# A causal decoder layer in float32: later gate/up tiles in pairs, two of eight k pairs by seven block products

## The chip, the cores and the metric

One core of a Trainium2 chip runs the whole program once. The metric is the device time of an execution in microseconds. Three timed runs of the kernel before gave 953.26, 953.99 and 954.17 us; their median is 953.99 us. The profile is of a further execution.

## The reference

One layer is computed for 256 tokens of width 2048, in float32: a sparse attention mixer, then a gated feed-forward part, each followed by a layer norm over a weighted residual (alpha = 2^0.25). The change concerns the feed-forward part:

```
x <- LN(alpha*x + mixer(x))
x <- LN(alpha*x + (silu(x @ w_gate) * (x @ w_up)) @ w_down)
x: 256 x 2048, w_gate, w_up: 2048 x 5632, w_down: 5632 x 2048
```

## The kernel before, in words

**Split products.** TensorE multiplies numbers of the reduced type fp32r. To keep float32 precision each operand is a high part (rounded to fp32r) plus a low part (the rest), and a product is three matmuls: high by high, high by weight low, low by weight high (`product`, L1324; L1327 is the matmul). The activations are split once and lie in `act_t` (index 0 high, 1 low). The weights are split as they stream in.

**The stream of halves.** Weights come from HBM in loads of 1 MB (128 partitions x 2048 floats) into a ring of four raw slots; SyncE issues them in order (`load`, L392, which waits until the low parts of the load four before are made). Each load is two halves of 1024 columns. For a half ScalarE makes the high part (`hi_loop`, L621 to L627, a copy into `w_hi`), VectorE the low part (`lo_loop`, L899 to L903, raw minus high, into `w_lo`), and TensorE multiplies. `w_hi` and `w_lo` are rings of four halves (RING = 4): ScalarE waits for TensorE to be done with the half four before (`pe_used`, or `ffn_full` for the last half of a tile), VectorE for ScalarE (`hi_done`), TensorE for VectorE (`lo_done`). Each engine takes its instructions strictly in the order of its program.

**Gate and up.** 5632 hidden columns are 22 tiles of 256 gate and 256 up columns, that is one bank of 512 columns for each of two token blocks t. A tile is 8 halves of two k tiles of 128 rows; a half is 2 k x 2 t x 3 = 12 matmuls of 128x512, a tile 96. Tile 0 is interleaved with the layer norm (`first_tile`); tiles 1 to 21 run in `ffn_tile` (L1497 on TensorE, L692 on ScalarE, L1055 on VectorE), the last 20 in a loop, alternating two pairs of banks of `acc`. After a tile ScalarE takes silu of the gate columns (`silu_step`, L684 to L686, into `sig`), VectorE multiplies by the up columns (`gate_up`, L1035 to L1037, into `hid`), turns it with 16 transposes of 32x128 in two groups of eight (`turn_hid`, L1039 to L1047), ScalarE makes the high part of the turned tile (`hid_hi`, L690) and VectorE the low part (`hid_lo`, L1051 to L1053). These steps of tile i stand written by hand between the splits of tile i+1:

```
def ffn_tile(i, c):                    # VectorE
    for h in range(TILE_HALVES):
        lo_loop(2 * R_FFN + TILE_HALVES * i + h, h % 2, h // 2)
        if h == 3:
            gate_up(i - 1, 1 - c)
            turn_hid(i - 1, (0, 1))
        if h == 4:
            turn_hid(i - 1, (2, 3))
        if h == 6:
            hid_lo(i - 1)
```

**Down.** `hid_t` (44 k tiles) is multiplied by `w_down` in four column groups of 24 halves, whose first eight are alternately of 2 and 1 k tiles; the residual and the second norm follow. The steps of tile 21 stand in the first seven halves. `diag` (L739) and the matmuls that wait for it (L1555) belong to the norm at the very end.

## Time and profile before

| what | value |
|---|---|
| timed runs | 953.26, 953.99, 954.17 us |
| span of the profiled execution | 952.0 us |
| TensorE busy | 946.2 us (99%) |
| VectorE busy | 633.8 us (67%) |
| ScalarE busy | 441.9 us (46%) |
| GpSimd busy | 40.9 us (4%) |
| read from HBM | 181.01 MB, 192 GB/s over the span |

The profiled execution's own time is its span plus what lies around it; the tables of the profile give the span, and the median of the timed runs is 2.0 us above it. In the profile PE is TensorE, PEld its weight loads, DVE VectorE, ACT ScalarE, POOL GpSimd and SP SyncE. A matmul's printed length is longer than its spacing from the next, since matmuls are pipelined.

### The profile page before, as it was taken

Reading aid. Unit: us, or ns where it says so; the run is one execution under the profiler, and the core shown is the slowest. Engines: PE = TensorE matmul, PEld = TensorE weight load, DVE = VectorE, ACT = ScalarE, POOL = GpSimd, SP = SyncE. Lnnn points to the kernel's source line nnn. Section 1 sums busy time; section 2 is a strip of 40 time slices with the busy share of each in tenths; the row PEclk is TensorE's granted clock in tenths of the full one; section 3 lists DMA queues with packets and bytes.
Section 4 is the critical chain, followed back from the end, with each engine's and each line's share of the span. In section 5 each row is a group of like instructions: output and inputs, shape, how many; then the busy total and the mean of one; then the engine's idle time right before and its main releaser. Section 6 shows DMA issues by size and latency. Waiting matters only on the chain.

```text
span 952.0 us, 12299 instructions
## 1 busy us (share of the span) xinstructions
PE 946.2 (99%) x4508; PEld 793.8 (83%) x4508; DVE 633.8 (67%) x1012; ACT 441.9 (46%) x573; POOL 40.9 (4%) x43
## 2 busy tenths in 40 slices
PE   9999999999999999999999999999999999999997
PEld 8999988888888888888888888888888888888885
DVE  6778566588776677777776776677775454554556
ACT  5676764362544444444444444444444343343450
POOL 0105530000000000000000000000000000000000
PEclk9999999999999999999999999999999999999999
DMA  9735225583365555554455555545457465464632
GB/s 365 318 140 177 97 82 185 209 347 142 108 219 204 180 203 190 186 209 178 176 184 211 204 193 185 210 178 194 181 209 291 141 232 188 160 237 156 225 129 88
DMA packets 28128, 183.57 MB, mean 193 GB/s; under 512 B 3136, under 2 KB 3648, under 8 KB 8640
## 3 DMA queue, kind: packets, MB, share of 16 engines
q1 hardware_dynamic: 28064, 183.12, 52.7%
q8 instruction: 22, 0.36, 0.2%
q14 instruction: 10, 0.08, 0.0%
q0 software_dynamic: 32, 0.00, 0.0%
HBM read 181.01 MB, written 2.10 MB: 192 GB/s over the span
## 4 chain that ended last, share of the span: by engine, by line
PE 99%; DVE 0%; ACT 0%; DVEq 0%; issue 0%; ACTq 0%
PE acc L1327 82%; PE acc L1265 5%; PE acc L1186 4%; PE acc L1464 2%; PE acc L1299 1%; PE tp L1378 1%; PE tp L1313 1%; PE tp L1391 1%; PE tp L1175 0%; PE tp L1404 0%; PE tp L1403 0%; PE tp L1402 0%; PE tp L1420 0%; PE acc L1555 0%; PE tp L1233 0%; DVE stats L1107 0%
## 5 line engine op out<-in xcount | busy, mean ns | idle before, releaser
L903 DVE TENSOR_TENSOR w_lo<-raw,w_hi 128x1024 fp32r<-128x1024 f32 (+1 forms) x283 | 335.3, 1194 | 242.4 <-ACT w_hi L627 240.6
L627 ACT ACTIVATE w_hi<-raw 128x1024 fp32r<-128x1024 f32 (+1 forms) x276 | 285.7, 1036 | 403.2 <-PE acc L1327 401.1
L1327 PE MATMUL acc<-w_hi,act_t 128*128 128x512 f32 x1344 | 413.9, 389 | 0.0
L1327 PEld LDWEIGHTS acc<-w_hi,act_t 128*128 128x128 f32 x1344 | 252.3, 188 | 52.5
L1327 PE MATMUL acc<-w_lo,act_t 128*128 128x512 f32 x672 | 261.4, 389 | 0.0
L1327 PE MATMUL acc<-w_hi,hid_t 128*128 128x512 f32 x672 | 207.2, 389 | 0.0
L1327 PEld LDWEIGHTS acc<-w_lo,act_t 128*128 128x128 f32 x672 | 126.1, 188 | 26.1
L1327 PEld LDWEIGHTS acc<-w_hi,hid_t 128*128 128x128 f32 x672 | 126.1, 188 | 26.1
L1327 PE MATMUL acc<-w_lo,hid_t 128*128 128x512 f32 x336 | 130.7, 389 | 0.0
L1047 DVE STREAM_TRANSPOSE turned<-hid 32x128 f32<-32x128 f32 x352 | 106.6, 303 | 5.6
L1327 PEld LDWEIGHTS acc<-w_lo,hid_t 128*128 128x128 f32 x336 | 63.1, 188 | 13.2
L1327 PE MATMUL acc<-w_hi,o_t 128*128 128x512 f32 x224 | 73.4, 398 | 0.0
L1327 PEld LDWEIGHTS acc<-w_hi,o_t 128*128 128x128 f32 x224 | 42.1, 188 | 8.6
L1327 PE MATMUL acc<-w_lo,o_t 128*128 128x512 f32 x112 | 43.6, 390 | 0.0
L779 DVE TENSOR_TENSOR w_lo<-raw,w_hi 128x1024 fp32r<-128x1024 f32 x24 | 29.1, 1219 | 7.7 <-ACT w_hi L489 7.7
L1265 PE MATMUL acc<-cq_t,w_hi 128*128 128x256 f32 x160 | 31.1, 289 | 0.0
L489 ACT ACTIVATE w_hi<-raw 128x1024 fp32r<-128x1024 f32 x24 | 25.0, 1051 | 3.9 <-DMA raw<-in_w_qidx 3.9
L1162 POOL TENSOR_SCALAR prob<-prob,row_inv 128x128 f32<-128x128 f32 (+1 forms) x24 | 25.2, 1063 | 26.7 <-DVE row_inv L877 26.7
L1265 PEld LDWEIGHTS acc<-cq_t,w_hi 128*128 128x128 f32 x160 | 25.2, 188 | 1.1 <-issue 1.0
L1327 PEld LDWEIGHTS acc<-w_lo,o_t 128*128 128x128 f32 x112 | 21.1, 188 | 4.1
L866 DVE TENSOR_TENSOR o_t<-tp,o_t 128x256 fp32r<-128x256 f32 x16 | 6.8, 425 | 25.1 <-ACT o_t L604 25.1
L1265 PE MATMUL acc<-cq_t,w_lo 128*128 128x256 f32 x80 | 22.5, 281 | 0.0
(179 smaller groups left out, 740.1 us busy)
## 6 DMA issues: line engine op xcount, KB each, us to landing
raw<-in_w_gu SPq DMA_DIRECT2D x88, 1024.0 KB, 4.8
raw<-in_w_down SPq DMA_DIRECT2D x32, 1024.0 KB, 4.6
raw<-in_w_out SPq DMA_DIRECT2D x16, 1024.0 KB, 4.8
raw<-in_w_down SPq DMA_DIRECT2D x16, 768.0 KB, 4.0
raw<-in_x_w SPq DMA_DIRECT2D x14, 552.0 KB, 7.1
raw<-in_w_uq SPq DMA_DIRECT2D x4, 1024.0 KB, 6.0
raw<-in_w_ukv SPq DMA_DIRECT2D x4, 1024.0 KB, 5.7
ln_rows<-in_ln_rows SPq DMA_DIRECT2D x4, 1024.0 KB, 7.3
```

The lines of the kernel that those rows point to most:

```text
L489: act.activation(split_place(v)[0][:, v % RING, :], raw[:, r % RING, half * HALF:(half + 1) * HALF], ACT.Copy).then_inc(hi_done, 1)
L627: act.activation(w_hi[:, (2 * slot + half) % RING, 0:n], raw[:, slot, first:first + n], ACT.Copy).then_inc(hi_done, 1)
L779: dve.tensor_tensor(w_lo[:, v % RING, :], raw[:, r % RING, half * HALF:(half + 1) * HALF], w_hi[:, v % RING, :], ALU.subtract).then_inc(lo ...
L903: dve.tensor_tensor(w_lo[:, h, 0:n], raw[:, slot, first:first + n], w_hi[:, h, 0:n], ALU.subtract).then_inc(lo_done, 1)
L1047: last = dve.transpose(dst[:, :, :, 32 * n:32 * n + 32], src[:, :, :, 32 * b:32 * b + 32])
L1162: pool.tensor_scalar(prob[:, s % 3, cols], prob[:, s % 3, cols], row_inv[:, (s + 1) % 2, t:t + 1], None, ALU.mult).then_inc(prob_done, 1)
L1186: last = pe.matmul(acc[:, 2 * t + b, 0:c1 - c0], x[:, tok], w[:, c0:c1], start=(k == 0 and x is hi_ and w is hi_), stop=(k == KD - 1 and x ...
L1265: last = pe.matmul(out, part[:, v % RING, e0:e0 + P], act_tiles[:, k, x, :], start=(half == 0 and k == 0 and x == 0 and part is hi_), stop ...
L1299: last = pe.matmul(acc[:, (m + t) % 4, :], ckv_t[:, k, x, t * P:(t + 1) * P], wp[:, v % RING, k * 512:(k + 1) * 512], start=(n == 0), stop ...
L1313: last = pe.matmul(tp[:, h % 4, c0:c0 + n], qidx_t[rows, h // 2, t * P:(t + 1) * P], kidx_t[rows, 0:n], start=True, stop=True)
L1327: last = pe.matmul(acc[:, bank0 + t, :], lhs[:, k, x, t * P:(t + 1) * P], part[:, w, n * GC:(n + 1) * GC], start=(start and x == 0 and par ...
L1464: done = pe.matmul(acc[:, bank, :], act_t[:, k, x, t * P:(t + 1) * P], parts[part][:, w, n * GC:(n + 1) * GC], start=((h, n, x, part) == ( ...
```

## The change

Tiles 2 to 21 are taken as ten pairs (tiles 2p and 2p+1, p from 1 to 10). Of a pair's 16 k tiles, 4 (two "quads" of two k tiles) are multiplied as 2x2 blocks: token block (2) x k tile (2) by k tile (2) x tile of the pair (2). The weight blocks B11, B21, B12, B22 of both quads lie in two raw slots, and seven products of block sums (the Strassen scheme in Winograd's form) give the four results that eight products gave. The other 12 k tiles are 12 "plain halves" of 12 matmuls: six for the first tile, six for the second. A product half is 2 quads x 3 = 6 matmuls into one bank.

- VectorE makes four weight sums per pair (`t_sum`) between the low parts, in place in the raw slots. ScalarE's split of a sum waits for it (`t_done`).
- Partial sums are passed between banks: ScalarE copies the running bank into three others (`seed`, one with sign -1), copies product 1's bank to `p5_s`, and VectorE adds or subtracts it in both banks of the second tile after plain half 4. TensorE waits for `seeded` before products 2, 4 and 6, and for `p5_added` before plain half 6.
- The activation sums S1 to S4 are made once, during tile 1, by six GpSimd operations and one ScalarE copy (`s_t`).
- `sig` is gone: silu writes into `hid`, and waits until the tile before is turned. The hid product of tile 2p now stands after plain half 9 of its own pair, its 16 transposes in plain halves 0 and 1 of the next pair (for the last pair, after halves 1 and 2 of down); those of tile 2p-1 in plain halves 3 and 4.
- Raw slots: 3 for plain loads, 2 for quads. The first quads are loaded when all of tile 1's low parts are made; later ones when the seven products of the pair before are split.
- The loops over tiles are written out. `diag` and the row tensors share a place with `p5_s`. The DMA scratch size is set to 1024.

The core of the diff (TensorE's, VectorE's and ScalarE's order for a pair, SyncE's loads):

```diff
+            def lo_pair(p):
+
+                second = banks_of(2 * p + 1)
+                lo_product(p, 0, B11)
+                t_sum(B11, B11, B12)
+                t_sum(B12, B12, B22)
+                lo_product(p, 1, B11)
+                t_sum(B11, B11, B22)
+                lo_product(p, 2, B11)
+                lo_product(p, 3, B21)
+                t_sum(B21, B11, B21)
+                lo_product(p, 4, B12)
+                lo_product(p, 5, B22)
+                lo_product(p, 6, B21)
+                for h in range(2 * PLAIN):
+                    lo_plain(p, h)
+                    if h == 0 and p > 1:
+                        turn_hid(2 * p - 2, (0, 1))
+                    if h == 1 and p > 1:
+                        turn_hid(2 * p - 2, (2, 3))
+                    if h == 2:
+                        if p > 1:
+                            hid_lo(2 * p - 2)
+                        gate_up(2 * p - 1)
+                    if h == 3:
+                        turn_hid(2 * p - 1, (0, 1))
+                    if h == 4:
+                        turn_hid(2 * p - 1, (2, 3))
+
+                        dve.wait_ge(p5_done, p)
+                        dve.wait_ge(*used_pair(p, 5))
+                        dve.tensor_tensor(second[:, 0, :], p5_s[:], second[:, 0, :], ALU.add).then_inc(p5_added, 1)
+                        dve.wait_ge(seeded, 3 * p)
+                        dve.tensor_tensor(second[:, 1, :], p5_s[:], second[:, 1, :],
+                                          ALU.subtract).then_inc(p5_added, 1)
+                    if h == 6:
+                        hid_lo(2 * p - 1)
+                    if h == 9:
+                        gate_up(2 * p)
...
+            def hi_pair(p):
...
+                hi_product(p, 0, B11)
+                act.wait_ge(t_done, 4 * (p - 1) + 1)
+                hi_product(p, 1, B11)
+                act.wait_ge(t_done, 4 * (p - 1) + 3)
+                hi_product(p, 2, B11)
+                hi_product(p, 3, B21)
+                act.wait_ge(ffn_hid, 2 * p - 1)
+                seed(p, 0, first[:, 0, :], 1.0)
+                hi_product(p, 4, B12)
+                hi_product(p, 5, B22)
...
+                act.wait_ge(*used_pair(p, 1))
+                act.activation(p5_s[:], tp[:, 2, :], ACT.Copy).then_inc(p5_done, 1)
+                seed(p, 2, second[:, 0, :], -1.0)
+                act.wait_ge(t_done, 4 * p)
+                hi_product(p, 6, B21)
+                hi_plain(p, 0)
+                seed(p, 4, first[:, 1, :], 1.0)
+                for h in range(1, 2 * PLAIN):
+                    hi_plain(p, h)
+                    if h == 2 and p > 1:
+                        hid_hi(2 * p - 2)
+                    if h == 2:
+                        silu_step(2 * p - 1)
+                    if h == 6:
+                        hid_hi(2 * p - 1)
+                    if h == 9:
+                        silu_step(2 * p)
...
+            def pair(p):
+
+                first, second = banks_of(2 * p), banks_of(2 * p + 1)
+                u, p5 = second[:, 1, :], tp[:, 2, :]
+                pe.wait_ge(ffn_hid, max(1, 2 * p - 2))
+                strassen(p, 0, "a11", u, True)
+                pe.wait_ge(s_lo, 1)
+                if p > 1:
+                    pe.wait_ge(p5_done, p - 1)
+                strassen(p, 1, "s1", p5, True)
+                pe.wait_ge(seeded, 3 * p - 2)
+                strassen(p, 2, "s2", u, False)
+                strassen(p, 3, "a12", first[:, 0, :], False)
+                pe.wait_ge(seeded, 3 * p - 1)
+                strassen(p, 4, "s3", u, False)
+                strassen(p, 5, "s4", second[:, 0, :], False)
+                pe.wait_ge(seeded, 3 * p)
+                strassen(p, 6, "a22", first[:, 1, :], False)
+                for h in range(PLAIN):
+                    plain(p, h, first)
+                pe.wait_ge(p5_added, 2 * p)
+                for h in range(PLAIN, 2 * PLAIN):
+                    plain(p, h, second)
...
+            def load_quads(p):
+
+                if p > 1:
+                    sp.wait_ge(lo_done, v_pair(p - 1, PRODUCTS))
+                for q in range(QUADS):
+                    if p == 1 and q == 0:
+                        sp.wait_ge(lo_done, V_FFN + 2 * TILE_HALVES)
...
-                act.activation(sig[:], acc[:, 2 * c:2 * c + 2, 0:FC], ACT.Silu).then_inc(ffn_sig, 1)
+                if i > 0:
+                    act.wait_ge(ffn_turned, i)
+                act.activation(hid[:], banks_of(i)[:, :, 0:FC], ACT.Silu).then_inc(ffn_sig, 1)
...
+                    if g == 0 and h in (1, 2):
+                        turn_hid(TILES - 2, ((0, 1), (2, 3))[h - 1])
                     if g == 0 and h == 3:
-                        gate_up(TILES - 1, 1)
+                        hid_lo(TILES - 2)
+                        gate_up(TILES - 1)
```

## Rows read from the trace of the kernel before

**Rows 1.** The page: head, and busy time of each engine.
```profile
span 952.0 us, 12299 instructions
PE 946.2 (99%) x4508; PEld 793.8 (83%) x4508; DVE 633.8 (67%) x1012; ACT 441.9 (46%) x573; POOL 40.9 (4%) x43
```
**Rows 2.** The page: chain that ended last, by line (engine, tile, line, share).
```profile
PE acc L1327 82%; PE acc L1265 5%; PE acc L1186 4%; PE acc L1464 2%; PE acc L1299 1%; PE tp L1378 1%; PE tp L1313 1%; PE tp L1391 1%; PE tp L1175 0%; PE tp L1404 0%; PE tp L1403 0%; PE tp L1402 0%; PE tp L1420 0%; PE acc L1555 0%; PE tp L1233 0%; DVE stats L1107 0%
```
**Rows 3.** Stretches: us; busy PE, PEld, DVE, ACT, POOL; clock, DMA share, GB/s.
```profile
262.00:266.00 4.00, 4.00 (x19) 3.33 (x18) 1.98 (x3) 1.59 (x2) 0.00 (x0) 1.00 1.00 381
...
269.80:717.00 447.20, 447.20 (x1975) 370.29 (x1974) 323.43 (x544) 197.72 (x208) 0.00 (x0) 1.00 0.54 194
...
720.00:929.00 209.00, 209.00 (x923) 173.05 (x923) 105.25 (x98) 87.00 (x88) 0.00 (x0) 1.00 0.52 188
...
945.80:949.00 3.20, 2.81 (x6) 1.04 (x6) 2.84 (x6) 0.06 (x1) 0.00 (x0) 1.00 0.35 131
```
**Rows 4.** Timeline of ACT, from 508.98: start, length, instruction, idle before.
```profile
508.98 1.06 ACT L627 ACTIVATE w_hi<-raw 128x1024 fp32r<-128x1024 f32 x1 [1.66 <-PE acc L1327]
509.95 0.58 ACT L686 ACTIVATE sig<-acc 128x512 f32<-128x512 f32 x1
511.70 1.06 ACT L627 ACTIVATE w_hi<-raw 128x1024 fp32r<-128x1024 f32 x1 [1.18 <-PE acc L1327]
```
**Rows 5.** Timeline of all engines over one half, from 500.40.
```profile
500.40 0.62 PE L1327 MATMUL acc<-w_hi,act_t 128*128 128x512 f32 x2
...
500.82 1.06 ACT L627 ACTIVATE w_hi<-raw 128x1024 fp32r<-128x1024 f32 x1 [1.66 <-PE acc L1327]
...
501.92 1.23 DVE L903 TENSOR_TENSOR w_lo<-raw,w_hi 128x1024 fp32r<-128x1024 f32 x1 [1.30 <-ACT w_hi L627]
```
**Rows 6.** Timeline of DVE, one tile's steps among the low parts, 315 to 327.
```profile
315.38 0.68 DVE L1037 TENSOR_TENSOR hid<-sig,acc 128x512 f32<-128x512 f32 x1
316.10 2.50 DVE L1047 STREAM_TRANSPOSE turned<-hid 32x128 f32<-32x128 f32 x8
318.62 1.23 DVE L903 TENSOR_TENSOR w_lo<-raw,w_hi 128x1024 fp32r<-128x1024 f32 x1
319.87 2.53 DVE L1047 STREAM_TRANSPOSE turned<-hid 32x128 f32<-32x128 f32 x8
322.44 2.36 DVE L903 TENSOR_TENSOR w_lo<-raw,w_hi 128x1024 fp32r<-128x1024 f32 x2
324.72 0.68 DVE L1053 TENSOR_TENSOR hid_t<-turned,hid_t 128x512 f32 x1
325.32 1.22 DVE L903 TENSOR_TENSOR w_lo<-raw,w_hi 128x1024 fp32r<-128x1024 f32 x1
```
**Rows 7.** Timeline of ACT and PE at the end, from 945.27.
```profile
945.27 0.40 ACT L739 ACTIVATE diag<-ident,small 128x128 f32<-128x128 f32 x1 [9.93 <-DVE small L945]
...
945.82 2.81 PE L1555 MATMUL acc<-ln_rows,diag 128*128 128x512 f32 x6 [1.67 <-ACT diag L739]
```
**Rows 8.** Groups by line and shape: count, busy us, mean ns, idle before.
```profile
L1153 POOL TENSOR_TENSOR more_lo<-raw,more_hi 128x1024 fp32r<-128x1024 f32 x4 | 9.6, 2398 | 41.5 <-DVE score L838 41.1
...
L498 ACT ACTIVATE q_t<-acc 128x512 f32<-128x512 f32 x8 | 4.8, 597 | 6.3 <-PE acc L1265 6.3
...
L937 DVE SCALAR_TENSOR_TENSOR acc<-xn,acc 128x512 f32<-128x512 f32 x1 | 0.7, 689 | 0.0
```
**Rows 9.** Timeline of DVE and of ACT around the end of tile 1.
```profile
260.81 1.22 DVE L903 TENSOR_TENSOR w_lo<-raw,w_hi 128x1024 fp32r<-128x1024 f32 x1
...
269.62 1.06 ACT L627 ACTIVATE w_hi<-raw 128x1024 fp32r<-128x1024 f32 x1 [1.66 <-PE acc L1327]
```
**Rows 10.** The page: DMA issues, count, KB each, us to landing.
```profile
raw<-in_w_gu SPq DMA_DIRECT2D x88, 1024.0 KB, 4.8
```
**Rows 11.** Timeline of PE at the start of the kernel, from 5.34.
```profile
5.34 1.05 PE L1186 MATMUL acc<-in_hi,in_lo 128*128 128x512 f32 x2
6.19 0.69 PE L1186 MATMUL acc<-in_lo,in_hi 128*128 128x512 f32 x2
```

More of the change, by code:

```diff
@@ L626, in hi_loop @@
                 act.wait_ge(*used)
-                act.activation(w_hi[:, (2 * slot + half) % RING, 0:n], raw[:, slot, first:first + n],
+                act.activation(w_hi[:, (2 * slot + half + shift) % RING, 0:n], raw[:, slot, first:first + n],
                                ACT.Copy).then_inc(hi_done, 1)
@@ L707, in down_half @@
+            tile_1()
+            for p in range(1, PAIRS):
+                hi_pair(p)
             def down_half(h, g):
@@ new lines, in factor, with strassen @@
+            def factor(q, what, x):
+                if what[0] == "s":
+                    return s_t[:, x, int(what[1]) - 1, q, :]
+                t, k = int(what[1]) - 1, int(what[2]) - 1
+                return act_t[:, 2 * q + k, x, t * P:(t + 1) * P]
+            def strassen(p, n, what, out, start):
+                v = v_pair(p, n)
+                pe.wait_ge(lo_done, v + 1)
+                for q in range(QUADS):
+                    for x, part in ((0, w_hi), (0, w_lo), (1, w_hi)):
+                        last = pe.matmul(out, factor(q, what, x), part[:, v % RING, q * GC:(q + 1) * GC],
+                                         start=(start and (q, x) == (0, 0) and part is w_hi),
+                                         stop=((q, x) == (QUADS - 1, 1)), skip_group_check=not start)
+                last.then_inc(pe_used, 1)
@@ new lines, in plain @@
+            def plain(p, h, out):
+                n = PRODUCTS + h
+                v, k0 = v_pair(p, n), PAIR_K + 2 * (h % PLAIN)
+                pe.wait_ge(lo_done, v + 1)
+                for m in range(2):
+                    for t in range(TOK):
+                        for x, part in ((0, w_hi), (0, w_lo), (1, w_hi)):
+                            last = pe.matmul(out[:, t, :], act_t[:, k0 + m, x, t * P:(t + 1) * P],
+                                             part[:, v % RING, m * GC:(m + 1) * GC], start=False,
+                                             stop=((h % PLAIN, m, x) == (PLAIN - 1, 1, 1)), skip_group_check=True)
+                last.then_inc(*((ffn_full, 1) if h % PLAIN == PLAIN - 1 else (pe_used, 1)))
@@ L1509, in _ @@
             first_tile()
-            ffn_tile(1, 1)
-            with pe.Fori(1, TILES // 2) as i:
-                ffn_tile(2 * i, 0)
-                ffn_tile(2 * i + 1, 1)
+            tile_1()
+            for p in range(1, PAIRS):
+                pair(p)
             def down_half(g, h, tokens):
-                parts = (down_hi, down_lo) if g == COL_GROUPS - 1 and h >= HELD + RING else (w_hi, w_lo)
+                late = g == COL_GROUPS - 1 and h >= HELD + RING
+                parts, w = ((down_hi, down_lo), h % RING) if late else ((w_hi, w_lo), (h + DOWN_POS) % RING)
@@ L1578 @@
     gate, up = (w[n].reshape(D, TILES, FC) for n in ("l0_ffn_gate", "l0_ffn_up"))
+    gu = k_tiles(np.stack([gate, up], axis=2).reshape(D, 2 * FFN), 2 * FC)
+    later = gu[2:].reshape(PAIRS - 1, 2, P, KD, 2 * FC)
+    quads = later[:, :, :, 0:PAIR_K].reshape(PAIRS - 1, 2, P, QUADS, 2, 2 * FC).transpose(0, 2, 3, 1, 4, 5)
+    plain = later[:, :, :, PAIR_K:].transpose(0, 2, 1, 3, 4).reshape(PAIRS - 1, P, -1)
     arrays = {
@@ L1585 @@
         "w_out": k_tiles(w["l0_w_out"], GC),
[L1586 removed]
+        "w_gu": gu[0:2],
+        "w_pairs": np.concatenate([quads.reshape(PAIRS - 1, P, -1), plain], axis=2),
         "w_down": k_tiles(w["l0_ffn_down"], GC),
```

249 lines of the change are left out of this document (193 added, 56 removed).

## The prediction

> **What bounds the kernel now.** I read the page first: the span is 952.0 us and TensorE is busy 99% of it [rows 1]. The chain that ended last is TensorE's for 82% of its length at one line, L1327, the three matmuls of a product [rows 2]. The table of stretches shows that the gate/up stretch (269.8 to 717) is 447.2 us with TensorE busy throughout, 1975 matmuls, clock 1.00, and VectorE 323.4 us (72%), ScalarE 197.7 us [rows 3]. One half (12 matmuls, 1024 raw columns) takes 2.72 us: ScalarE's splits start 2.72 us apart (508.98 and 511.70) [rows 4], so one matmul has 0.2267 us. So only TensorE's work counts today. The other engines have slack because of the ring of four split halves: the split of a half starts when TensorE is done with the half four before it.
>
> The timeline gives the hand-over [rows 5]. A half's last matmul starts at 500.40, the next half's first at 500.63 (0.62 us for two), ScalarE's split starts at 500.82, 0.19 after that boundary, lasts 1.06, and VectorE's low part starts 0.04 after it, at 501.92, for 1.23 us. Back to back, one VectorE operation follows the last earlier than its printed length [rows 6]: low part 1.14 us ((324.72-322.44)/2), but 1.25 where a transpose follows (318.62 to 319.87); hid product 0.72; eight transposes 2.52 and the other eight 2.57; hid low part 0.60. On ScalarE a follower starts 0.09 before the printed end (509.95 against 508.98+1.06) [rows 4]. How soon TensorE restarts after a wait shows only at the end: ScalarE's diag ends at 945.67, the matmul starts at 945.82, 0.15 us [rows 7]. I take 0.15; the bounds are 0.05 and 0.30.
>
> The median of the three timed runs, 953.99 us, stands 2.0 us above this profiled span [rows 1]. I work in the profile's time and add the 2.0 at the end.
>
> **TensorE's part.** Ten pairs of tiles. A pair had 192 matmuls; now 7 products x 2 quads x 3 = 42 and 12 plain halves x 12 = 144, together 186. Six matmuls x 0.2267 = 1.36 us a pair, 13.6 us in all. That is the most the change can bring.
>
> **What the others get, per pair.** VectorE: 16 low parts become 19, plus four weight sums of 128x1024 (two operands in SBUF and 1024 columns, as the low part has, so 1.23 us alone and 1.14 back to back [rows 5, 6]), plus two adds of P5 over a bank (L937, 0.689 [rows 8], so 0.72). Sum: 23 x 1.14 + 4 x 0.11 (in front of transposes) + 2 x 5.09 + 2 x 0.72 + 2 x 0.60 + 2 x 0.72 = 40.9 us. TensorE's pair is now 186 x 0.2267 = 42.2 us. VectorE rises from 72% to 97% of TensorE's time. That alone would fit; its order does not.
>
> ScalarE: three more splits and four copies out of a bank (three seeds and P5). A copy from PSUM to SBUF is 0.597 us (L498) [rows 8]. The seeds write to PSUM, which no row shows from ScalarE; bounds 0.50 and 0.70, I take 0.60. The Trainium skill says of this (ScalarE: Activation LUTs, "Step-by-step: what each stage is for") that ScalarE reaches PSUM faster than SBUF; it gives no time. By it the seeds would be at the low bound and my sum 2.3 us lower; no row here shows it.
>
> **A pair in the steady state** (pairs 2 to 10). Zero is the start of product 0 on TensorE. It runs without a wait: VectorE has caught up by the end of the previous pair, so product 0's split starts when plain half 8 is done, 8.16 - 0.19 us ahead. The chain from there (low part, sum, split, low part, two sums, split, low part) takes 3.5 us a link and ends at -5.6, -2.1 and 1.4, in time for 0, 1.36 and 2.72. Then:
> - ScalarE: after product 0 ends (1.36) the first seed starts at 1.55, and back to back follow splits 4 and 5, the P5 copy, the second seed and split 6: 1.55 + 0.51 + 0.96 + 0.96 + 0.51 + 0.51 = 5.00, end 6.06. VectorE's low part of product 6 starts at 6.10.
> - VectorE from there has no pause: low parts of product 6 and plain 0 (1.14 + 1.25), eight transposes of tile 2p-2, the first of the pair before (2.52), plain 1 (1.25), eight more (2.57), plain 2 (1.14), its hid low (0.60), the hid product of tile 2p-1 (0.72), plain 3 (1.25), eight transposes of that (2.52), plain 4 (1.25), eight more (2.57), two P5 adds (1.44), plain 5 (1.23). That is 21.45 us, end 27.55; TensorE can start plain 5 at 27.70.
> - TensorE without waits: 7 x 1.36 + 5 x 2.72 = 23.12. So it stands still 4.58 us a pair, in pieces: some 0.15 before plain 1, 1.1 before plain 2, 0.8 before plain 4, 2.5 before plain 5.
> In the kernel before, one tile's cluster (from 315.4 to 325.3, 9.9 us with its three low parts [rows 6]) fell on four halves, 10.9 us, once per eight, and the ring hid it. Now two clusters stand in the first five plain halves, and the seven products ahead of them give TensorE only 1.36 us of work each for one low part (and often a sum). Net: 4.58 - 1.36 = +3.22 us, nine times: **+29.0**.
>
> **The first pair.** Its quads are loaded only when the last low part of tile 1 is done (slot 3 is shared): that ends at 260.81+1.22 = 262.03 [rows 9]. One 1 MB load lands after 4.8 us [rows 10]; at 381 GB/s, the rate of a full DMA stretch [rows 3], its bytes take 2.75, so two land after 4.8+2.75 = 7.55 us, at 269.6. Split, low part: 271.98; TensorE starts at 272.1. Tile 1 ends at 269.43 (split at 269.62 less 0.19) [rows 9]: 2.7 us of waiting. There is no lead now, so each link of the chain shows: product 1 waits 2.15 (sum 1.23, split 1.06, low part 1.23 and hand-overs against 1.36), product 2 waits 2.34 (two operations more), product 4 waits 0.51. Together 7.7 - 1.36 = **+6.3**. It has no deferred tile to turn, so nothing follows.
>
> **Down.** Two tiles' transposes now fall in its first seven halves instead of one: some 5 us more of VectorE work with ring lead in front: **+0.8** by the same count, bounds 0 and 2.
>
> **Costed at nothing.** GpSimd's sums, once: its 1024-column operation is 2.4 us [rows 8], two of these and four of a quarter size, about 8 us, beside 21.8 us of tile 1; ScalarE's s split (1.06) lies in slack there. If that cover failed, product 1 waits once, 1 or 2 us. Silu's wait for the turning of the tile before (hid is reused): ScalarE waits behind the transposes, up to 5 us in plain 2 to 3, but its splits of plain 3 to 5 (ended by about 19) are still ahead of VectorE, which is the late one. SP: loads of a slot are asked four halves ahead (10.9 us against 4.8), and the quads a whole plain stage ahead. Written-out loops: the down stage is written out on TensorE already and runs 923 matmuls in 209.0 us, 0.2264 each, as the looped gate/up (447.2/1975 = 0.2264) [rows 3]. Scratch size, moved diag and row tensors: nothing.
>
> **Sum:** 29.0 + 6.3 + 0.8 = +36.1; span 988.1, time 990.1 us. Bounds: restart 0.05 or 0.30, -1.1 or +1.7; PSUM copies 0.50 or 0.70, -2.3 or +2.7; P5 adds 0.80 us, +1.4; down -0.8 or +1.2; loads slower than 381 GB/s at the first pair or in plain halves +2 to +4; copies so short that the ring alone (product 6's slot, free at 4.08) holds back the last product, up to -4. Range 981 to 1000.
>
> **Rivals.**
> - Other side: the ring's lead hides VectorE's piece after all, and only the 13.6 us saved and the first pair's cost are left: 990.1 - 9 x 4.58 - 0.8 = 948.1 us. Its place is product 6 to plain 5, its price 4.58 us a pair. It decides once the 21.45 us piece is 4 us shorter, which is where 9 stalls and 7.7 us of pair 1 meet the 13.6 us. For it: total VectorE work, 40.9, is still below 42.2. Against: each duration of the piece is in the rows, and they add up for the cluster before to within 0.1 us. Chance 0.04.
> - Half hidden: VectorE enters the piece some 2 us earlier than I say, 990.1 - 18 = 972. Against: split 6 cannot start before product 2 is done (4.08 + 0.19), 0.7 us earlier at most. Chance 0.04.
> - TensorE's clock falls in the stalls of 2.5 us. The stretches show clock 1.00, the last one too, which follows a wait of 1.67 us for diag [rows 3, 7]. But matmuls at the start stand 0.425 us apart (5.34 to 6.19 for two) against 0.2267 later [rows 11]. If a half after each stall ran at that spacing: 12 x 0.2 = 2.4 us, ten times, 1014 us. The Trainium skill (TensorE: Matmul & The Clock Gate, Part 1) says the engine's clock is halved after idleness and restored by activity; no row here shows whether stalls this long suffice. Chance 0.06.
> - The change does not save its matmuls (a product costs more than six slots). Up to 1.36 us a pair would vanish in the stall behind it; the time stays 990. It is no case of its own.
> The main case has 0.86.
>
> **Numbers.** 0.2% (2 us) is about what a measurement of this kernel can tell. Faster 0.04 (the first rival), same 0.01, slower 0.95. The range takes the main case's bounds and leaves out the rivals.
>
> **What the profile after would show.** TensorE matmuls 60 fewer; its idle, some 49 us, put down to VectorE's low parts, the longest piece (about 2.5 us) before each pair's sixth plain half; a pair's period 42.16 + 4.58 = 46.7 us; sums of 1.22 us; seeds near 0.6; VectorE without a gap for 21 us a pair; a wait of some 2.7 us before the first product. I am wrong if the period is below 43.5, if the sums or seeds differ by over 0.2 us, or if TensorE waits for DMA in the steady state.

## The result and the profile after

| | before | after |
|---|---|---|
| median of the timed runs | 954.02 us (953.26 to 954.17) | 1003.24 us (1002.95 to 1004.98) |
| span of the profiled execution | 952.0 us | 1000.9 us |
| TensorE busy | 946.2 us | 957.7 us |
| VectorE busy | 633.8 us | 729.1 us |

The change is slower: ratio 1.0523 (95% interval 1.0508 to 1.0538), 49.2 us where the prediction had 36.1. The sign and the place were right; the time, 1003.2, lies 3 us above the range.

The page of the kernel after: head, busy times, and the chain that ended last, by engine.

```profile
span 1000.9 us, 11621 instructions
...
PE 957.7 (96%) x4448; PEld 790.0 (79%) x4448; DVE 729.1 (73%) x1102; ACT 483.5 (48%) x644; POOL 53.1 (5%) x49
...
PE 71%; DVE 23%; ACT 4%; issue 1%; DMA 1%; DVEq 0%; SPq 0%; ACTq 0%
```

Against [rows 1, 2]: TensorE has 60 matmuls fewer, as it should, and yet is "busy" for longer (957.7 us). That is the first sign that its clock was not always full: at a lower clock the same matmul takes longer. VectorE holds 23% of the chain that ended last, where it had next to nothing.

The waits of the kernel after (engine, tile, line, whom it waited for: us in all, times, longest).

```profile
PEld acc L1799 <- DVE w_lo L1265: 41.5, 36, 2.6
...
PE acc L1799 <- DVE w_lo L1265: 28.5, 27, 2.1
...
ACT w_hi L836 <- DMA raw<-in_w_pairs: 11.0, 1, 11.0
...
PE acc L1786 <- DVE w_lo L1258: 6.0, 2, 5.7
```

36 is four waits in each of nine pairs, before plain halves 1, 2, 4 and 5 (the first, 0.18 us, is too short to show in the matmuls' 27). L1799 is a plain half's matmul, L1265 its low part. The other two lines are the first pair's: one wait for a DMA, and TensorE's 5.7 us behind it.

Stretches of the kernel after, with the columns of [rows 3]: the gate/up pairs, down, part of the first pair, and five microseconds around plain half 5 of pair 2.

```profile
270.00:717.00 447.00, 414.25 (x1728) 331.61 (x1728) 374.79 (x553) 221.58 (x256) 0.00 (x0) 0.96 0.45 171
...
766.00:978.00 212.00, 212.00 (x937) 175.54 (x936) 108.15 (x101) 88.13 (x89) 0.00 (x0) 1.00 0.53 193
...
274.00:276.00 2.00, 1.41 (x3) 1.16 (x4) 2.00 (x3) 0.39 (x1) 0.00 (x0) 0.50 0.00 0
...
278.00:280.00 2.00, 1.61 (x6) 1.05 (x6) 1.07 (x1) 0.90 (x1) 0.00 (x0) 1.00 0.00 0
...
349.00:350.00 1.00, 1.00 (x4) 0.81 (x5) 1.00 (x2) 0.00 (x0) 0.00 (x0) 0.79 0.21 49
350.00:351.00 1.00, 1.00 (x4) 0.81 (x3) 1.00 (x3) 0.00 (x0) 0.00 (x0) 0.50 0.93 311
351.00:352.00 1.00, 1.00 (x4) 0.72 (x4) 1.00 (x2) 0.00 (x0) 0.00 (x0) 0.50 0.99 418
352.00:353.00 1.00, 1.00 (x4) 0.81 (x3) 0.88 (x1) 0.00 (x0) 0.00 (x0) 0.50 1.08 369
353.00:354.00 1.00, 1.00 (x6) 0.83 (x5) 0.00 (x0) 0.43 (x1) 0.00 (x0) 1.00 0.86 295
```

In 447 us of pairs TensorE is without work for 32.8 us, where [rows 3] have none; down is as full as it was. Behind the start of plain half 5, at 348.93, the granted clock falls to 0.50 (1.2 GHz) and stays there until 353: three whole microseconds and 0.42 of the one with a mean of 0.79, some 3.4 us.

TensorE's timeline in the kernel after: first the first pair, then pair 2. The bracket is the idle time ahead of the instruction and what ended it.

```profile
274.59 0.76 PE L1786 MATMUL acc<-w_hi,act_t 128*128 128x512 f32 x1 [5.74 <-DVE w_lo L1258]
...
278.08 0.47 PE L1786 MATMUL tp<-w_hi,s_t 128*128 128x512 f32 x1 [0.59 <-DVE w_lo L1258]
...
281.64 0.50 PE L1786 MATMUL acc<-w_hi,s_t 128*128 128x512 f32 x1 [1.96 <-ACT acc L851]
...
321.81 0.39 PE L1786 MATMUL tp<-w_hi,act_t 128*128 128x512 f32 x1
...
336.62 0.39 PE L1799 MATMUL acc<-w_hi,act_t 128*128 128x512 f32 x1
337.79 0.50 PE L1799 MATMUL acc<-w_hi,act_t 128*128 128x512 f32 x1 [0.79 <-DVE w_lo L1265]
...
343.14 0.39 PE L1799 MATMUL acc<-w_hi,act_t 128*128 128x512 f32 x1
343.78 0.50 PE L1799 MATMUL acc<-w_hi,act_t 128*128 128x512 f32 x1 [0.26 <-DVE w_lo L1265]
...
346.41 0.39 PE L1799 MATMUL acc<-w_hi,act_t 128*128 128x512 f32 x1
348.93 0.50 PE L1799 MATMUL acc<-w_hi,act_t 128*128 128x512 f32 x1 [2.13 <-DVE w_lo L1265]
...
350.26 0.63 PE L1799 MATMUL acc<-w_lo,act_t 128*128 128x512 f32 x1
350.68 1.06 PE L1799 MATMUL acc<-w_hi,act_t 128*128 128x512 f32 x2
```

A matmul is due 0.227 us after the last one's start. So the first matmul of plain half 2 came 0.94 us late (337.79 less 336.85), that of plain half 4 0.41 and that of plain half 5 2.29: the printed brackets are shorter, since the printed end is later than 0.227, and the brackets of the weight loads (41.5 us in the waits) are longer. Behind the last pause the matmuls stand 0.42 us apart (350.26 to 350.68).

VectorE's timeline in the kernel after: its end of tile 1, then its unbroken piece in pair 2.

```profile
243.24 8.36 DVE L1091 TENSOR_TENSOR w_lo<-raw,w_hi 128x1024 fp32r<-128x1024 f32 x4 [0.26 <-ACT w_hi L755]
...
260.85 2.88 DVE L1241 TENSOR_TENSOR hid_t<-turned,hid_t 128x512 fp32r<-128x512 f32 x1
263.65 1.30 DVE L1091 TENSOR_TENSOR w_lo<-raw,w_hi 128x1024 fp32r<-128x1024 f32 x1
...
325.42 3.71 DVE L1258 TENSOR_TENSOR w_lo<-raw,w_hi 128x1024 fp32r<-128x1024 f32 x3
329.04 1.22 DVE L1265 TENSOR_TENSOR w_lo<-raw,w_hi 128x1024 fp32r<-128x1024 f32 x1
330.18 2.50 DVE L1235 STREAM_TRANSPOSE turned<-hid 32x128 f32<-32x128 f32 x8
...
338.26 0.68 DVE L1225 TENSOR_TENSOR hid<-hid,acc 128x512 f32<-128x512 f32 x1
338.85 1.22 DVE L1265 TENSOR_TENSOR w_lo<-raw,w_hi 128x1024 fp32r<-128x1024 f32 x1
339.99 2.50 DVE L1235 STREAM_TRANSPOSE turned<-hid 32x128 f32<-32x128 f32 x8
...
347.65 2.36 DVE L1265 TENSOR_TENSOR w_lo<-raw,w_hi 128x1024 fp32r<-128x1024 f32 x2
```

The piece runs from product 6's low part (the third of the three at 325.42; its split ends at 327.87) to the end of plain 5's at 348.88, without a gap: TensorE's matmul starts 0.05 us later.

ScalarE's timeline in the kernel after: the split of product 0 in pairs 1, 2 and 3. GpSimd's: one of the quarter-size sums, and the low part of the sums.

```profile
272.13 1.06 ACT L836 ACTIVATE w_hi<-raw 128x1024 fp32r<-128x1024 f32 x1 [11.03 <-DMA raw<-in_w_pairs]
...
313.93 1.06 ACT L836 ACTIVATE w_hi<-raw 128x1024 fp32r<-128x1024 f32 x1 [1.74 <-PE acc L1799]
...
361.84 1.06 ACT L836 ACTIVATE w_hi<-raw 128x1024 fp32r<-128x1024 f32 x1 [1.74 <-PE tp L1799]
```

```profile
245.55 1.60 POOL L1420 TENSOR_TENSOR s_sum<-x_t 128x256 f32<-128x256 f32 x1
...
260.23 2.95 POOL L1427 TENSOR_TENSOR s_t<-s_sum,s_t 128x1024 fp32r<-128x1024 f32 x1 [8.04 <-ACT s_t L831]
```

A pair's period is the distance of two such splits, 47.91 us (eight of them, 313.93 to 697.02, have a mean of 47.89). The last low part of tile 1 ends at 264.95, where [rows 9] have 262.03.

### The profile page after: what moved, and what is told of

It reads as the page before. It is cut to its first block, busy times and chain, and to the rows that moved or that the text cites. A ratio compares the mean times of both kernels' runs of the same rounds, so it can differ in the third digit from the quotient of the medians.

```text
span 1000.9 us, 11621 instructions
## 1 busy us (share of the span) xinstructions
PE 957.7 (96%) x4448; PEld 790.0 (79%) x4448; DVE 729.1 (73%) x1102; ACT 483.5 (48%) x644; POOL 53.1 (5%) x49
## 4 chain that ended last, share of the span: by engine, by line
PE 71%; DVE 23%; ACT 4%; issue 1%; DMA 1%; DVEq 0%; SPq 0%; ACTq 0%
PE acc L1590 32%; PE acc L1799 14%; DVE turned L1235 10%; PE tp L1799 8%; DVE w_lo L1265 6%; PE acc L1528 5%; PE acc L1449 4%; ACT w_hi L836 3%; DVE w_lo L1091 2%; DVE w_lo L1258 2%; PE acc L1727 2%; PE acc L1562 1%; PE tp L1641 1%; PE acc L1786 1%; DVE hid_t L1241 1%
## 5 line engine op out<-in xcount | busy, mean ns | idle before, releaser
L1799 PE MATMUL acc<-w_hi,act_t 128*128 128x512 f32 x720 | 242.0, 410 | 28.5 <-DVE w_lo L1265 28.5
L1091 DVE TENSOR_TENSOR w_lo<-raw,w_hi 128x1024 fp32r<-128x1024 f32 (+1 forms) x123 | 144.6, 1184 | 120.6 <-ACT w_hi L755 119.6
L1799 PEld LDWEIGHTS acc<-w_hi,act_t 128*128 128x128 f32 x720 | 142.1, 197 | 71.6 <-DVE w_lo L1265 41.5
L755 ACT ACTIVATE w_hi<-raw 128x1024 fp32r<-128x1024 f32 x116 | 115.6, 1001 | 160.3 <-PE acc L1590 147.9
L1265 DVE TENSOR_TENSOR w_lo<-raw,w_hi 128x1024 fp32r<-128x1024 f32 x120 | 145.1, 1223 | 42.4 <-ACT w_hi L845 41.4
L845 ACT ACTIVATE w_hi<-raw 128x1024 fp32r<-128x1024 f32 x120 | 122.7, 1053 | 84.2 <-PE acc L1799 67.8
L1799 PE MATMUL acc<-w_lo,act_t 128*128 128x512 f32 x360 | 146.0, 406 | 0.0
L836 ACT ACTIVATE w_hi<-raw 128x1024 fp32r<-128x1024 f32 x70 | 72.9, 1057 | 75.6 <-DVE raw L1270 48.5
L1258 DVE TENSOR_TENSOR w_lo<-raw,w_hi 128x1024 fp32r<-128x1024 f32 x70 | 83.8, 1222 | 34.9 <-ACT w_hi L836 33.7
L1799 PEld LDWEIGHTS acc<-w_lo,act_t 128*128 128x128 f32 x360 | 71.2, 198 | 14.2
L1799 PE MATMUL tp<-w_hi,act_t 128*128 128x512 f32 x240 | 74.7, 389 | 0.0
L1799 PEld LDWEIGHTS tp<-w_hi,act_t 128*128 128x128 f32 x240 | 45.0, 188 | 9.4
L1270 DVE TENSOR_TENSOR raw<-raw 128x1024 f32<-128x1024 f32 x40 | 47.9, 1219 | 0.0
L1799 PE MATMUL tp<-w_lo,act_t 128*128 128x512 f32 x120 | 46.7, 389 | 0.0
```

What stands on the lines that cost most here:

```text
L755: act.activation(w_hi[:, (2 * slot + half + shift) % RING, 0:n], raw[:, slot, first:first + n], ACT.Copy).then_inc(hi_done, 1)
L836: act.activation(by_quad(w_hi[:, v_pair(p, n) % RING, :]), quad(block), ACT.Copy).then_inc(hi_done, 1)
L845: act.activation(w_hi[:, v_pair(p, n) % RING, :], raw[:, slot, h % 2 * HALF:(h % 2 + 1) * HALF], ACT.Copy).then_inc(hi_done, 1)
L1091: dve.tensor_tensor(w_lo[:, h, 0:n], raw[:, slot, first:first + n], w_hi[:, h, 0:n], ALU.subtract).then_inc(lo_done, 1)
L1258: dve.tensor_tensor(by_quad(w_lo[:, v % RING, :]), quad(block), by_quad(w_hi[:, v % RING, :]), ALU.subtract).then_inc(lo_done, 1)
L1265: dve.tensor_tensor(w_lo[:, v % RING, :], raw[:, h // 2 % PAIR_RING, h % 2 * HALF:(h % 2 + 1) * HALF], w_hi[:, v % RING, :], ALU.subtract) ...
```

## The experiments

Theory A is the prediction's: VectorE's order, not its total, holds TensorE up in each pair. Two more came from the profile after: the clock falls behind the longest pause, and GpSimd delays VectorE ahead of the first pair. Each kernel is the changed one with the edit shown, cuts in it marked by dots; the time before, run on the same chips, was 953.84 (e1, e2, e4, e5), 953.37 (e3, e6, e7, e9) and 953.56 us (e8, e10). A "piece" is a run of VectorE's operations without a gap, a "split" ScalarE's copy that makes a high part, and a pair's period is the distance of the splits of product 0 in two pairs running. The time is a median; spans and rows are those of one profiled execution, and executions of a kernel lie up to some 3 us apart.

### TensorE turns one tile of each pair

```diff
-                    if h == 0 and p > 1:
-                        turn_hid(2 * p - 2, (0, 1))
-                    if h == 1 and p > 1:
-                        turn_hid(2 * p - 2, (2, 3))
...
+                    if h == 10:
+                        pe.wait_ge(ffn_hid, 2 * p + 1)
+                        pe.wait_ge(ffn_lo, 2 * p - 1)
+                        for c in range(2):
+                            for t in range(TOK):
+                                last = pe.transpose(tp[:, 3, (2 * c + t) * P:(2 * c + t + 1) * P],
+                                                    hid[:, t, c * P:(c + 1) * P], ident[:])
...
```

> The first tile of each pair is turned by TensorE (four transposes, about 0.44 us, before plain half 10) instead of by VectorE (16 transposes, 5.1 us, in plain halves 0 and 1 of the next pair). Theory A (VectorE's piece of 21.5 us against 17.0 us of TensorE's): the piece becomes 16.2 us, no stall is left in pairs 2 to 10, period 42.2 + 0.44 = 42.6 us, clock 1.00; only the first pair's cost and 13.6 - 4.4 us of gain remain: 952 to 957 us. Theory B (ScalarE's copies between banks or the hand-overs of the products hold TensorE up): a period of 45 us or more, 975 us or more.

957.63 us, ratio 1.0040 (1.0026 to 1.0055): 45.6 us less than the changed kernel, and just above what was expected. Some 14.5 of the 45.6 are the clock's (below), which has no pause to fall behind here. A stretch of this kernel, where the one after had gaps:

```profile
320.00:720.00 400.00, 400.00 (x1783) 331.14 (x1782) 330.84 (x430) 220.22 (x254) 0.72 (x1) 1.00 0.53 196
```

TensorE is full and at full clock; a pair takes 42.66 us (splits of product 0 at 315.05 and 357.71), against 43.52 before (192 x 0.2267) and a reckoned 42.16 for 186 matmuls alone. VectorE lost 47.7 us of work (681.4 us busy).

### The weight sums left out

```diff
-                t_sum(B11, B11, B12)
-                t_sum(B12, B12, B22)
...
-                act.wait_ge(t_done, 4 * (p - 1) + 1)
...
```

All four sums and the three waits for them go. The products then multiply plain blocks, so that the kernel's output is no longer the layer's; it only serves to time the rest.

> The four weight sums of each pair are left out with their waits, so the products multiply plain blocks. Theory A (the pair's period is set by VectorE's unbroken piece from product 6 to plain half 5, and the sums lie before it, where the lead of the ring takes them): only the first pair, which has no lead, gets shorter, by 2 to 4 us; 999 to 1001 us, period of a later pair still 47.9 us. Theory B (VectorE's total work is what counts, so 4 x 1.14 = 4.6 us a pair come back): period about 43.3 to 44, 958 to 963 us.

998.78 us, ratio 1.0468 (1.0451 to 1.0486). VectorE lost 43.6 us of work (685.5 us busy), nearly as much as above, and the time fell by 4.5 us instead of 45.6. In the profiled execution, whose span is 2.6 us below the changed kernel's (998.3 and 1000.9), this is the first pair (pair 2's first split at 311.21 instead of 313.93); the period stayed (311.21, 359.14, 407.05: 47.9). The two quickest of its four executions, 997.6 us each, had a mean granted clock of 0.985 for 0.981; that points to the clock for the rest. Had VectorE's total been the bound, this kernel's period would have fallen by some 4 us too. What counts is whether the work lies in the piece from product 6 to plain half 5.

### The same transposes on VectorE, two halves from the end of the pair

```diff
-                    if h == 0 and p > 1:
-                        turn_hid(2 * p - 2, (0, 1))
...
-                        turn_hid(2 * p - 2, (2, 3))
...
+                    if h == 10:
+                        turn_hid(2 * p, (0, 1))
+                    if h == 11:
+                        turn_hid(2 * p, (2, 3))
...
```

> VectorE still makes all 32x128 transposes, but those of a pair's first tile stand after plain halves 10 and 11 of the same pair instead of 0 and 1 of the next; ScalarE and VectorE split it one half earlier. VectorE's total work per pair stays 40.9 us. Theory A (the order, not the total, holds TensorE up): the piece before plain half 5 fits, in exchange products 2 and 4 of the next pair wait some 0.9 and 0.5 us; period about 43.6 instead of 47.9, clock 1.00 in the pairs, time 962 to 966 us. Theory B (VectorE's total of 40.9 us plus its unavoidable pauses is the bound): period 46 or more, 985 us or more.

966.37 us, ratio 1.0132 (1.0116 to 1.0147): 36.9 us less with not one operation fewer (VectorE busy 727.3 us), and just above what was expected. The period is 43.83 (316.06, 359.89). No wait for a plain half's low part is left. The 1.67 us over 42.16 now lie at the products, which VectorE enters late, so that the seeds come late; the timeline of the weight loads in pair 2 of this kernel shows it:

```profile
327.60 0.19 PEld L1786 LDWEIGHTS tp<-w_hi,s_t 128*128 128x128 f32 x1 [1.20 <-ACT acc L851]
330.89 0.19 PEld L1786 LDWEIGHTS tp<-w_hi,s_t 128*128 128x128 f32 x1 [0.69 <-ACT tp L851]
```

### Spare matmuls in the longest pause

```diff
+                    if h == 5 and p > 1:
+                        for _ in range(8):
+                            pe.matmul(tp[:, 3, :], act_t[:, KD - 1, 0, 0:P],
+                                      act_t[:, 0, :, :].rearrange("p x s -> p (x s)"), start=True, stop=True)
```

> Eight extra 128x512 matmuls into an unused bank stand before plain half 5 of pairs 2 to 10, 1.8 us of work in the 2.3 us in which TensorE stands still there; the result is not touched. Theory A (beside VectorE's piece, TensorE's clock falls to half after that wait and costs 1.2 us a pair): the granted clock stays 1.00 in pairs 2 to 10, the period falls from 47.9 to 46.7 us, the time by about 10 us to 993. Theory B (the low clock costs nothing, since VectorE is the one that is late): clock 1.00 but period and time unchanged, 1003. If the matmuls only delay plain half 5: slower by up to 9 x 1.8 = 16 us.

990.78 us, ratio 1.0389 (1.0371 to 1.0406): 12.5 us less with 72 matmuls more. That is somewhat more than expected, and nothing of VectorE's was touched: plain half 5 starts 27.11 us after product 0 here and 27.12 in the kernel after. TensorE's timeline at plain half 5 of pair 2:

```profile
349.49 0.50 PE L1799 MATMUL acc<-w_hi,act_t 128*128 128x512 f32 x1 [0.31 <-DVE w_lo L1265]
```

ScalarE's timeline in this kernel, with product 0's split of pairs 2 and 3, gives the period, 46.28 us:

```profile
314.50 1.06 ACT L836 ACTIVATE w_hi<-raw 128x1024 fp32r<-128x1024 f32 x1 [1.74 <-PE acc L1799]
...
360.78 1.06 ACT L836 ACTIVATE w_hi<-raw 128x1024 fp32r<-128x1024 f32 x1 [1.74 <-PE tp L1799]
```

So the clock cost 1.6 us a pair (47.89 less 46.28), and the pauses by themselves 4.12 (46.28 less 42.16). Nine times 1.6 are 14.5 us, and the median fell by 12.5, for the first pair takes back a part: its half clock, which the spare matmuls don't touch, lasts longer in some executions than in others. The profiled execution of this kernel took 989.23 us at a mean granted clock of 0.997, the three others 990.72 to 990.90 at 0.993.

With three spare matmuls (0.68 us) instead of eight:

> As the kernel with eight extra matmuls before plain half 5, but three: 0.7 us of work, so TensorE still stands still for about 1.6 us there. Theory A (the clock falls only after the long wait; the 1.2 us waits before plain half 2 brought no fall): granted clock stays near 1.00 in pairs 2 to 10, time near the 991 us of eight. Theory B (a wait of 1.6 us is enough for the fall): the clock falls as before, time near 1003.

990.74 us, ratio 1.0386 (1.0370 to 1.0402), period 46.27 (315.93, 362.19). The same gain: TensorE then pauses for up to 1.9 us by its weight loads (2.6 in the kernel after), and the clock stays at 1.00 in pairs 2 to 10. Here the first pair shows where the rest of the 14.5 us went: pair 2's first split is 2.0 us later than in the kernel after (315.93 and 313.93).

### The first quads loaded during tile 1

```diff
+TILE_1_SLOTS = (4, 0, 1, 2)
...
-                    if p == 1 and q == 0:
-                        sp.wait_ge(lo_done, V_FFN + 2 * TILE_HALVES)
+                    if p == 1:
+                        sp.wait_ge(lo_done, V_FFN + TILE_HALVES + 2 * q)
...
-                    sp.wait_ge(lo_done, V_FFN + TILE_HALVES + 2 * n + 2)
+                    sp.wait_ge(lo_done, V_FFN + TILE_HALVES + 2 * (n + 1) + 2)
...
+                    load_quads(p)
                     load_plain(p, 0)
                     load_plain(p, 1)
                     load_plain(p, 2)
-                    load_quads(p)
...
```

> Tile 1's loads go to slots 4, 0, 1, 2, so that slots 3 and 4 are free for the first pair's quads while tile 1 runs; nothing else changes. Theory A (the first pair's waits come from the late load of the quads and the lack of lead behind it, with the half clock after a 6 us wait): all waits of pair 1 go, 8 to 11 us in all, 992 to 995 us. Theory B (the first pair's wait comes from the activation sums that GpSimd makes, done at 263.2): product 1 still waits, and less than 4 us come back.

994.14 us, ratio 1.0427 (1.0409 to 1.0444): 9.1 us less, as expected; but not all waits of the first pair are gone. Those of products 0 and 1 are; product 2 still waits 1.74 us for a seed and product 4 0.31 us for a low part. Pair 2's first split comes 7.7 us sooner (306.21 for 313.93), so this much of the first pair's cost was the late load, and some 2.6 us of waiting stay (product 0 at 269.32, that of pair 2 at 314.09: 44.77 us against 42.16). The span of the profiled execution is 11.0 us below the changed kernel's; the other 3.2 us are the clock's, which two pairs were spared. Its pair 2 took 46.28 us and its pair 3 47.88 (splits at 306.21, 352.49, 400.37), behind the same pause:

```profile
341.19 0.50 PE L1808 MATMUL acc<-w_hi,act_t 128*128 128x512 f32 x1 [2.12 <-DVE w_lo L1274]
...
387.47 0.80 PE L1808 MATMUL acc<-w_hi,act_t 128*128 128x512 f32 x1 [2.13 <-DVE w_lo L1274]
```

```profile
341.00:343.00 2.00, 1.81 (x8) 1.51 (x9) 2.00 (x4) 0.11 (x1) 0.00 (x0) 1.00 0.45 74
...
388.00:390.00 2.00, 2.00 (x6) 1.55 (x5) 2.00 (x3) 0.00 (x0) 0.00 (x0) 0.50 0.81 221
```

The first block is TensorE's timeline, the second the stretches behind. One pause left the clock at 1.00, the other, of the same length, halved it. Pair 7 was spared too (its pause reads 2.13 us), the other seven were not. The length of a pause alone doesn't settle it.

### The low part of the activation sums on VectorE

```diff
-            pool.wait_ge(s_hi, 1)
-            pool.tensor_tensor(s_t[:, 1, :, :, :], s_sum[:], s_t[:, 0, :, :, :], ALU.subtract).then_inc(s_lo, 1)
...
+                dve.wait_ge(s_hi, 1)
+                dve.tensor_tensor(s_t[:, 1, :, :, :], s_sum[:], s_t[:, 0, :, :, :], ALU.subtract).then_inc(s_lo, 1)
```

> The low part of the activation sums is made by VectorE after tile 1's last low part, in a stretch where it waits for the quads, instead of by GpSimd in the middle of tile 1. Theory A (while GpSimd's operation runs, 260.2 to 263.2, VectorE's two operations take 2.9 and 1.3 us instead of 0.7 and 1.2, and the first quads are asked that much later): VectorE's hid low part is back at 0.69 us, tile 1's last low part ends 2 to 2.5 us earlier, the first pair starts that much earlier, time about 1001. Theory B (the two do not touch each other, the hid low part waited for something else): durations and time unchanged, 1003.

1002.57 us, ratio 1.0512 (1.0496 to 1.0528): only 0.7 us less where about 2 were expected, a miss. The mechanism itself showed. VectorE's timeline in this kernel:

```profile
261.17 0.68 DVE L1241 TENSOR_TENSOR hid_t<-turned,hid_t 128x512 fp32r<-128x512 f32 x1
261.78 1.22 DVE L1091 TENSOR_TENSOR w_lo<-raw,w_hi 128x1024 fp32r<-128x1024 f32 x1
```

0.68 us again instead of 2.88, the last low part of tile 1 ends at 263.00 instead of 264.95, and product 0 starts at 272.84 instead of 274.59. But pair 2's first split is at 313.94, as before (313.93). The stretches of this kernel say where the 1.75 us went:

```profile
274.00:276.00 2.00, 1.74 (x5) 0.84 (x3) 2.00 (x2) 0.92 (x1) 0.00 (x0) 0.50 0.00 0
...
282.00:284.00 2.00, 2.00 (x6) 1.52 (x6) 2.00 (x2) 1.38 (x3) 0.00 (x0) 0.50 0.00 0
```

The clock was at 0.50 until 284, in the kernel after only until 278. To test this, 16 spare matmuls went ahead of the first pair's product 0 in e3_vec_s:

```diff
+                if p == 1:
+                    for _ in range(16):
+                        pe.matmul(tp[:, 3, :], act_t[:, KD - 1, 0, 0:P],
+                                  act_t[:, 0, :, :].rearrange("p x s -> p (x s)"), start=True, stop=True)
                 strassen(p, 0, "a11", u, True)
```

> e3_vec_s with 16 spare matmuls into an unused bank ahead of the first pair's product 0, some 3.6 us of work in the 3.65 us in which TensorE waited there. Theory (the half clock after that wait gave back what the earlier quads had gained): the granted clock stays at 1.00 from 269 to 285, the waits for VectorE in the first pair grow to the predicted 2.15, 2.34 and 0.51 us, and the first pair takes 42.2 + 5.0 = 47.2 us where e3_vec_s took 49.1; the time falls by some 1.9 us, to 1000.7 (1000.0 to 1001.5). Rival (the half clock lay in waits that were there anyway, and something else held e3_vec_s back): 1002.6, within 0.5.

999.62 us, ratio 1.0485 (1.0471 to 1.0499), a little below the range expected: 2.95 us below e3_vec_s by the medians and 1.8, near the 1.9 expected, by the spans of the profiled executions (999.2 and 1001.0). The stretch of this kernel:

```profile
269.00:284.00 15.00, 10.95 (x47) 8.14 (x46) 11.19 (x10) 8.56 (x11) 0.00 (x0) 1.00 0.05 23
```

Full clock throughout, product 0 at 273.20, pair 2's first split at 312.40, that is 39.20 us later; e3_vec_s took 41.10 and the kernel after 39.34. In the profiled execution of e3_vec_s the half clock had given the gain back. Whether the earlier start made it last so long there stays open, for how long it lasts also differs between kernels that are the same up to that point. Product 0 to pair 2's split took 39.34 us in the kernel after and in e2_fill, 40.47 in e9_fill3 and 40.62 in e7_turn_early, with the clock at 0.50 until about 278 in the first two and until about 286 in the others.

### The parts together

TensorE turns a tile of each pair, the first quads load early, and the sums' low part is VectorE's (the edits of e4_pe_turn, e5_early_quads and e3_vec_s):

> All three together: TensorE turns the first tile of each pair, tile 1's loads leave slots 3 and 4 free for the first quads, VectorE makes the low part of the activation sums. Theory A: no wait is left between 250 and 700, clock 1.00, and the time is 954 - 13.6 (60 matmuls fewer) + 4.4 (ten times 0.44 us of transposes) = 945 us, +-2. Theory B (something of the pairs' form costs beside these three): 950 us or more.

946.72 us, ratio 0.9931 (0.9917 to 0.9944): 6.7 us less than the kernel before in the same comparison, 0.7%. First the busy times of its page, then its stretch of pairs:

```profile
PE 937.9 (99%) x4488; PEld 786.1 (83%) x4488; DVE 680.5 (72%) x943; ACT 486.5 (51%) x644; POOL 50.2 (5%) x48
```

```profile
270.00:717.00 447.00, 446.12 (x1986) 368.75 (x1985) 368.32 (x476) 246.44 (x283) 0.72 (x1) 1.00 0.54 200
```

A pair takes 42.63 us (347.79, 390.42). The same with VectorE's early turning in place of TensorE's:

> The early turning of the kernel e7_turn_early (966.4 us, period 43.8), the early quads of e5_early_quads (9.1 us less than the changed kernel) and s's low part on VectorE, together; TensorE turns nothing. Theory A (costs in series, the steady state and the first pair apart from each other): 966.4 - 9.1 = 957.3, and 0 to 2 less for s: 957 us, 955 to 958.5, the period staying 43.8. Rival (the first pair's gain is taken back by VectorE's lag, as the clock took it back in e3_vec_s): 960 to 966.

956.41 us, ratio 1.0030 (1.0018 to 1.0041), 46.8 us less than the changed kernel with all of its VectorE work, and GpSimd's low part on top; only the order and the raw slots changed. The costs of the steady state and of the first pair add to within 1 us (966.37 less 9.1 is 957.3). Its period is 43.8; the 1.2 us a pair to e6_all's 42.63 lie at products 2 and 4, as in e7_turn_early.

## Why the prediction was right or wrong

In spans, 1000.9 less 952.0 is +48.9 us, against +36.1:

| part | predicted | measured | how |
|---|---|---|---|
| VectorE's piece, 9 pairs | +29.0 | +24.8 | 9 x (4.12 - 1.36) |
| the clock behind it, 9 pairs | 0 | +14.5 | 9 x (47.89 - 46.28) |
| first pair | +6.3 | +8.9 | pair 2's product 0 at 321.81; before it would be 269.43 + 43.52 = 312.95. Tile 1 ended 0.7 us sooner in the execution after, which is counted in |
| down and the end | +0.8 | +0.7 | the rest; directly +0.8, below |

**TensorE's saving.** Right: 60 matmuls fewer, 186 in a pair, and e4_pe_turn shows that they are worth their time once nothing else waits: a pair, with four transposes more, takes 42.66 us against 43.52.

**VectorE's piece.** The mechanism was right, and e1, e4 and e7 show it: 43.6 us of VectorE work outside the piece cost 4.5 us, 47.7 us inside it 45.6 (with the clock's share), and moving that work without removing any gives 36.9. The size was 0.46 us a pair too large. The piece's entry was exact (product 6's low part 6.10 us after product 0 began). Its length was 20.97 us where the prediction had 21.45: a low part in front of eight transposes is followed after 1.14 (329.04 to 330.18, 338.85 to 339.99) and only one between two groups of transposes after 1.26; the hid product behind hid's low part takes 0.59, not 0.72; the two P5 adds 1.33, not 1.44. The restart took 0.05, the low end of its bounds. So plain half 5 starts 27.12 us after product 0 (348.93 less 321.81), 0.58 sooner than the 27.70 predicted. Against that, the first matmul behind a pause is followed after 0.34 us and not 0.23, a cost that stood nowhere in the sum; only the one at plain half 5 adds to the pair, 0.11 us, since the others lie ahead of a start that VectorE sets. The pauses come to 0.94, 0.41 and 2.29 us, at the plain halves foretold (some 1.1, 0.8 and 2.5).

**The clock: the step that failed.** The prediction had it as a rival with 0.06, 2.4 us for each of ten pauses, and left it out of the range. It was no alternative to the main case but an addition to it: the main case's own pause of 2.5 us sets it off. In the profile after it fell in all nine pairs, for some 3.4 us each, and cost 1.6 us a pair, less than the 2.4 of the rival; e2_fill and e9_fill3 take it away without touching VectorE. 14.5 us are more than the whole error, 12.8 in spans: without the clock the sum would have come out 1.7 us too high, 4.2 too high for the piece and 2.6 too low for the first pair, which partly cancel by luck. The reason against it was the wait of 1.67 us at full clock [rows 7], which is shorter than the pause it was held against; nothing in the rows spoke for a full clock behind 2.5 us. The Trainium skill (TensorE: Matmul & The Clock Gate, Part 1) says that the monitor behind the clock runs on by itself, so that the same activity can have another effect from one execution to the next. The executions of e2_fill (mean granted clock 0.997 and 0.993) agree with it, and the two pauses of 2.12 and 2.13 us in e5_early_quads fit it; no run here tests it further.

**The first pair.** The wait for the DMA was foreseen, and the quads needed 7.1 us from the issue at 264.99, against 7.55. But they were issued 2.9 us later than predicted, since tile 1's last low part was. So the first product began 2.5 us later than predicted (274.59 and 272.1), which is nearly the whole miss of this term. This is the entry "GpSimd's sums, costed at nothing": it asked what happens if the sums come late, not whom they disturb. A quarter-size operation takes 1.60 us, not a quarter of 2.4. And while GpSimd works, VectorE's operations stretch: four low parts 8.36 us where before three took 3.50 and one 1.23, and hid's low part 2.88 instead of 0.68. e3_vec_s takes GpSimd's 2.95 us operation away, and the 0.68 is back. Counted from tile 1's first low part, the last one ends after 21.71 us in the kernel after, 19.43 in e3_vec_s and 18.06 in the kernel before. So 2.3 us are shown to be that operation's; the other 1.4 appear while GpSimd's first five operations run, and no run takes those away. The Trainium skill states it (SBUF — State Buffer, "Who interferes with whom"): a VectorE instruction with two inputs in SBUF contends with a GpSimd instruction that reads SBUF. Each low part is such an instruction, and the 2.88 us beside 0.68 agree; the rule spoke against this part of the change and belonged in the prediction. Of the waits behind product 0, that of product 1 was shorter than predicted in the kernel after (0.59 against 2.15), because TensorE at half clock used the time up: at full clock, in e10_first_fill, its bracket reads 1.82. Product 2's reads 1.96, and 1.93 in e10_first_fill, against 2.34: the clock has no part in that, and the sum had it too large.

**Down.** Right. From its first to its last product of hid it takes 239.93 us (752.70 to 992.63), 239.14 before (704.62 to 943.76), and 239.13 or 239.14 in e4_pe_turn, e6_all, e7_turn_early and e8_all_vec_turn, where no tile is left over to be turned there. The 0.8 us lie in its first halves; from 766 on it is full at full clock (1.00, 212.00 of 212.00).

**The copies into PSUM.** The seeds took 0.58 to 0.60 us by shape, as assumed, and the P5 copy into SBUF 0.587. The rule of the Trainium skill that the prediction weighed (ScalarE: Activation LUTs, "Step-by-step: what each stage is for"), ScalarE being quicker into PSUM, doesn't show in these rows, and the measurement decides: the low bound that it spoke for was not reached.

## What to carry to other kernels

When an engine's total load goes from 72% to 97% of the bound, lay its operations out in order and look for the longest unbroken piece between two hand-overs: here some 45 us of VectorE work cost 4.5 us in one place and 46 in another, and 37 of those 46 came back by moving it. Where the forecast itself has TensorE pausing again and again for as long as here (2.3 us), count the half clock in the sum or at least in the range; a few spare matmuls in the pause are a cheap test, and can be a remedy. Before giving GpSimd sums "beside" other work, ask which VectorE operations run meanwhile with two inputs in SBUF.
